# Band queries stored backwards in place of a flipped bias table, and reciprocal sums spread by GpSimd and transposes

## The chip, the cores and the metric

One core of a Trainium2 chip runs the whole kernel. The metric is the device time of one execution in microseconds (us); lower is better. The engines are named as in the profile: PE (TensorE), DVE (VectorE), ACT (ScalarE), POOL (GpSimd) and SP (SyncE, which here only issues DMAs).

## The reference, cut to what matters

The computation is two transformer blocks on 512 tokens of width 1024, all in float32. The first block has an MLA attention and a banded attention, gates, an output projection and a mixture of experts. The second has a windowed attention of 16 heads and a state-space scan. The change touches the softmax of all attentions and the relative bias of the banded one:

```
rel = (arange(64)[:, None] + 512) - arange(576)[None, :]
bias = rel_table[:, clip(rel, -256, 256) + 256]
sc = einsum('bqhd,bkhd->bhqk', q_chunk, k_band) * d ** -0.5 + bias
p = softmax(sc, axis=-1)
out = einsum('bhqk,bkhd->bqhd', p, v_band)
```

Query row q of the bias is the row before it shifted by one place, so a table with overlapping rows can be read straight from one vector.

## The kernel before, in words

Each engine has its own instruction list, written out by hand; they meet at semaphores, and an engine runs its own list strictly in order. DMAs are issued by SP for weights, and by ACT and POOL for the rest. Time runs through these stages: projections of the first block (`PE_S1`, then `PE_U`), the first attention, gates, output projection, router, mixture of experts, the projections of the second block, the second attention, convolution and state-space scan, output.

**An attention** is `attend(groups)`, with one copy in each engine's list. The first call does groups 0 (banded) and 1 (MLA), the second groups 2 and 3 (the 16 windowed heads). A group has 8 heads, taken as 4 pairs; a pair is 4 units n, one for each block of 128 queries, in the order t = 3, 0, 2, 1. A unit handles both heads of the pair and only (t+1)*128 keys, so unit n with n % 4 == 0 is the widest. For a unit:

- PE `scores(n)` (line 759) multiplies queries and keys into PSUM.
- DVE `bias_max` (line 1701) adds the bias and takes the row maximum.
- ACT `soft` (line 1336) takes the exponential and the row sums.
- PE `turn(n)` (line 769) transposes the probabilities, DVE and ACT `evict_pt` (lines 1709 and 1348) copy them to SBUF, and PE `values(n)` (line 782) multiplies them with the values.

PE issues turn(n), values(n-1), scores(n+2) in each round. When a pair is finished, DVE `invert` (line 1715) takes the reciprocals of its 8 columns of row sums, one round into the next pair. PE `spread` (line 793) then turns them into a full 128x512 tile in PSUM, by 8 matmuls: a column of reciprocals, broadcast over 64 columns, is the stationary operand and the identity moves. It is issued after scores(n+2) of the round with n % 4 == 1, or, for the last pair of a call, after everything else. DVE `normalise` (line 1721) multiplies the evicted output (ACT `evict_o`, line 1341) with it. The score and value matmuls of the next stage wait for `o_ready`.

**The bias table of group 0.** ACT's DMA at line 1400 reads it from DRAM with overlapping rows in the order of memory, so its partitions come in reverse order. PE multiplies each head's 128x512 tile with a flip matrix (line 865), DVE copies the result back (line 1845), and POOL writes the mask corner (line 2455). PE begins the attention when all eight are done. Before its own attention starts, DVE takes two weight remainders, `lo(M_G)` and `lo(M_G + 1)` (line 1675), and ACT the two rounded parts, `hi(M_G)` and `hi(M_G + 1)` (line 1323), of the first two gate tiles.

The first round of the attention also holds 16 small matmuls of the router (line 802), put after scores(0) and scores(1) and before turn(0); DVE adds their result in round 1.

After the first attention ACT (line 1410) and DVE (line 1856) split its eight output tiles into rounded part and remainder, which PE needs from line 888 on. After the second one ACT copies `RA` to `RC_r` (line 1537), POOL takes the remainders (line 2479), and PE's next column (line 663) waits for each. POOL's list during the second attention builds the biases of group 3 (lines 2488 and 2489), two heads per pair.

Of the kernel before, what the change touches and what calls it, by code (L numbers as in the profile page):

```python
# [19 lines left out]
F32 = mybir.dt.float32  # L20
# [52 lines left out]
def build(nc, xT_d, vec_d, rows_d, pos_d, rel_d, wr_d, wdt_d, pre_d, moe_d, post_d, out_d):  # L73
    ctx = ExitStack()
    with ctx:
# [32 lines left out]
        flip = sb("flip", [P, P])  # L108
# [169 lines left out]
        r_full = sem("r_full")  # L278
        o_raw = sem("o_raw")
# [58 lines left out]
        flip_full = sem("flip_full")  # L338
        flip_ev = sem("flip_ev")
# [289 lines left out]
        def _(pe):  # L629
# [114 lines left out]
            def attend(groups):  # L744
# [41 lines left out]
                def spread(pair):  # L786
                    pe.wait_ge(rs_ready, pair + 1)
                    if pair:
                        pe.wait_ge(o_ready, pair)
                    for t in range(TT):  # L790
                        for s in range(2):
                            r = pair_sums(rsinv, pair)[:, 2 * t + s:2 * t + s + 1].to_broadcast([P, 64])
                            last = mm(ps[7][64 * s:64 * s + 64, t * P:(t + 1) * P], r, ident[:, :], start=True, stop=True)
                    last.then_inc(r_full, 1)
# [66 lines left out]
            pe.wait_ge(bias_in, 16)  # L861
            for h in range(HG):
                if h >= 2:
                    pe.wait_ge(flip_ev, h)
                mm(ps[4 + h % 2][:, :], flip[:, :], bias_hc[:, h, :], start=True, stop=True).then_inc(flip_full, 1)
            pe.wait_ge(flip_ev, HG + 1)
# [365 lines left out]

        def s1_dst(i):
# [7 lines left out]
            if i < 8:  # L1241
                return [(qbT[:, i - 4, :], b[:, :])], 0.125
            if i < 12:
                return [(kbT[:, i - 8, :], b[:, :])], 1.0
            raise ValueError(i)

# [31 lines left out]
        def _(act):  # L1278
# [46 lines left out]
            def attend(groups):  # L1325
# [24 lines left out]
                for n in range(first, last_n):  # L1350
# [3 lines left out]
                    if n > first:  # L1354
                        evict_pt(n - 1)
                evict_pt(last_n - 1)
# [45 lines left out]
            hi(M_G)  # L1402
            hi(M_G + 1)
# [4 lines left out]
            for k in range(KT):  # L1408
                act.wait_ge(o_ready, PAIRS + k + 1 if k < PAIRS else 2 * PAIRS)
                A(REr[:, k, :], RH[:, k, :], ACT.Copy).then_inc(oab_hi, 1)  # L1410
# [244 lines left out]
        def _(dve):  # L1655
# [33 lines left out]
            def attend(groups):  # L1689
# [33 lines left out]
                for n in range(first, last_n):  # L1723
# [9 lines left out]
                    if n % TT == TT - 1 and n > first + TT:  # L1733
                        normalise(n // TT - 1)
                evict_pt(last_n - 1)
# [107 lines left out]
            for h in range(HG):  # L1843
                dve.wait_ge(flip_full, h + 1)
                v.tensor_copy(bias_hc[:, h, :], ps[4 + h % 2][:, :]).then_inc(flip_ev, 1)
            lo(M_G)
            lo(M_G + 1)
# [4 lines left out]
            for k in range(KT):  # L1852
# [3 lines left out]
                v.tensor_tensor(RFr[:, k, :], RH[:, k, :], REr[:, k, :].bitcast(F32), ALU.subtract).then_inc(oab_lo, 1)  # L1856
# [552 lines left out]
        def _(pool):  # L2409
# [3 lines left out]
            def link(ins):  # L2413
# [14 lines left out]
            g.memset(flip[:, :], 0.0).then_inc(flip_ev, 1)  # L2428
            pool.wait_ge(flip_ev, 1)
            link(g.affine_select(out=flip[:, :], in_=flip[:, :], compare_op=ALU.not_equal, fill=1.0, base=1 - P,  # L2430
                                 pattern=[[1, P]], channel_multiplier=1))
# [22 lines left out]
            pool.wait_ge(flip_ev, HG + 1)  # L2454
            g.memset(bias_hc[0:64, :, 448:512], NEG).then_inc(bias_ok, 1)
# [3 lines left out]
            for i in range(MAX_OVER + 1):  # L2459
                g.dma_start(exp_d[SURPLUS_ROW + i * P:SURPLUS_ROW + (i + 1) * P, :],  # L2460
                            SQ[:, :, :].rearrange("p a b -> p (a b)")).then_inc(zero_out, 16)
            pool.wait_ge(rows_ok, 1)
# [22 lines left out]
            for h in range(2 * HG):  # L2485
                if h >= HG:
                    pool.wait_ge(biased, 2 * NU + (h - HG) // 2 * 2 * TT + 2 * TT)
                link(g.tensor_scalar(RG[:, h % HG, :], delta, -float(2.0 ** (-8.0 * (h + 1) / 16)), None, ALU.mult))
                g.tensor_tensor(RG[:, h % HG, :], RG[:, h % HG, :], lnm, ALU.add).then_inc(bias_ok, 1)
            pool.wait_ge(s_full, 4 * NU)  # L2490
# [143 lines left out]
```

## Time and profile before

| What | Value |
|---|---|
| Median of 3 runs | 1323.54 us (1323.48 to 1325.14) |
| Span of the profiled execution | 1319.3 us |
| Time of the profiled execution itself | not given beside its span |
| Median minus span | 4.24 us |
| PE busy | 1231.7 us, 93% of the span |
| DVE, ACT, POOL busy | 48%, 35%, 13% |
| Line 865 (flips), PE | 181.20 to 188.89 us of the span |
| Line 793 (spreads), PE | 256 records in 16 spreads |

The profile is of one execution. Busy times of PE are modelled at their ends, so that neighbouring matmuls overlap in it; the pace is read from the starts of successive rows. A row of PE ahead of which there is no bracket had no idle time before it. One float32 matmul leaves two records, a transpose one.

### The profile page before, as it was taken

What the parts mean: (1) busy time and instruction counts of PE and PEld (TensorE: products, weight loads), DVE (VectorE), ACT (ScalarE), POOL (GpSimd) and SP (SyncE); (2) the same over time, 40 slices, a digit from 0 to 9 for tenths busy, and PEclk for the clock granted to TensorE, in tenths of its full rate; (3) what the DMA queues carried; (4) which work ended last, traced back from release to release, by engine and by line L of the source; (5) the groups of instructions that cost most, each with busy time, mean ns of one, the idle gap of its engine ahead of it and who ended that gap; (6) DMA issues with size and microseconds to landing.
All of it is one profiled execution on the core that took longest, in us unless ns stands there. A gap on an engine that the chain in (4) does not pass through costs nothing.

```text
span 1319.3 us, 17760 instructions
## 1 busy us (share of the span) xinstructions
PE 1231.7 (93%) x6946; PEld 873.0 (66%) x6946; DVE 636.4 (48%) x1180; ACT 460.8 (35%) x833; POOL 169.6 (13%) x136
## 2 busy tenths in 40 slices
PE   4899999999999989999989799999998999999995
PEld 1676566678887755444445268897656788787783
DVE  1654366554445454311111266424654675958545
ACT  3324226642222241111111252123664366564314
POOL 1200010000000000000000200700503018622003
PEclk9899999999999999999999799999999999999998
DMA  9555342113332299999999923322001222112201
GB/s 355 208 205 176 112 155 92 59 34 98 98 98 91 103 407 408 412 411 412 411 411 405 411 81 96 96 74 87 1 1 39 90 81 64 49 52 92 88 24 64
DMA packets 61633, 219.37 MB, mean 166 GB/s; under 512 B 6368, under 2 KB 6760, under 8 KB 61552
## 3 DMA queue, kind: packets, MB, share of 16 engines
q1 hardware_dynamic: 55440, 198.86, 41.4%
q10 hardware_dynamic: 3664, 10.47, 2.1%
q0 software_dynamic: 2448, 8.91, 1.7%
q8 instruction: 56, 0.92, 0.3%
q14 instruction: 25, 0.20, 0.0%
HBM read 203.52 MB, written 14.70 MB: 165 GB/s over the span
## 4 chain that ended last, share of the span: by engine, by line
PE 79%; DMA 7%; DVE 4%; ACT 4%; issue 4%; POOL 1%; SPq 0%; ACTq 0%; DVEq 0%; POOLq 0%
PE ps L663 12%; PE ps L664 12%; PE ps L665 12%; PE ps L961 6%; PE ps L942 4%; DMA ring<-in_w_moe 4%; PE ps L982 3%; PE ps L759 3%; PE ps L782 3%; PE ps L769 3%; PE ps L704 2%; PE ps L706 2%; PE ps L705 2%; PE ps L730 1%; DMA RG<-expert_rows,small 1%
## 5 line engine op out<-in xcount | busy, mean ns | idle before, releaser
L1675 DVE TENSOR_TENSOR ring_r<-ring,ring_r 128x1024 fp32r<-128x1024 f32 x115 | 143.7, 1253 | 198.3 <-ACT ring_r L1323 197.6
L1323 ACT ACTIVATE ring_r<-ring 128x1024 fp32r<-128x1024 f32 x116 | 121.2, 1052 | 204.6 <-PE ps L665 166.8
L663 PE MATMUL ps<-RB_r,ring_r 128*128 128x512 f32 x320 | 126.9, 396 | 1.1 <-DVE RH L1721 1.1
L665 PE MATMUL ps<-RB_r,ring_r 128*128 128x512 f32 x320 | 124.6, 389 | 0.0
L663 PE MATMUL ps<-RC_r,ring_r 128*128 128x512 f32 x224 | 91.1, 407 | 4.6 <-POOL RD_r L2479 3.7
L665 PE MATMUL ps<-RC_r,ring_r 128*128 128x512 f32 x224 | 87.8, 392 | 0.0
L664 PE MATMUL ps<-RD_r,ring_r 128*128 128x512 f32 x224 | 87.7, 392 | 0.0
L664 PE MATMUL ps<-RG_r,ring_r 128*128 128x512 f32 x208 | 81.1, 390 | 0.0
L1968 DVE TENSOR_SCALAR RH<-ps,small 128x256 f32<-128x256 f32 x72 | 31.5, 480 | 87.2 <-PE ps L942 87.0
L961 PE MATMUL ps<-ring,RH 128*64 128x512 f32 x308 | 73.3, 595 | 0.0
L2472 POOL DMA_INDIRECT RC<-expert_rows,small x4 | 3.8, 958 | 535.4 <-POOLq L2467 534.5
L663 PEld LDWEIGHTS ps<-RB_r,ring_r 128*128 128x128 f32 x320 | 60.1, 188 | 16.7 <-issue 4.5
L942 PE MATMUL ps<-RD_r,RC_r 128*128 128x256 f32 x288 | 67.6, 288 | 1.2 <-DVE RD_r L1948 1.2
L665 PEld LDWEIGHTS ps<-RB_r,ring_r 128*128 128x128 f32 x320 | 60.1, 188 | 12.8
L942 PE MATMUL ps<-RD_r,RG_r 128*128 128x256 f32 x288 | 66.1, 283 | 0.4 <-DVE RG_r L1957 0.4
L942 PEld LDWEIGHTS ps<-RD_r,RC_r 128*128 128x128 f32 x288 | 52.9, 191 | 13.4 <-issue 13.4
L1336 ACT ACTIVATE SB<-ps,small 128x512 f32<-128x512 f32 (+1 forms) x64 | 40.1, 630 | 43.8 <-DVE small L1701 40.3
L663 PEld LDWEIGHTS ps<-RC_r,ring_r 128*128 128x128 f32 x224 | 42.2, 188 | 19.0 <-POOL RD_r L2479 5.0
L704 PE MATMUL ps<-ring_r,RB_r 128*128 128x256 f32 x192 | 54.5, 284 | 0.0
L706 PE MATMUL ps<-ring_r,RB_r 128*128 128x256 f32 x192 | 54.3, 283 | 0.0
L2056 DVE TENSOR_TENSOR RB<-RB,ps 128x256 f32<-128x256 f32 x17 | 7.1, 420 | 95.9 <-ACT RB L1449 90.0
L942 PEld LDWEIGHTS ps<-RD_r,RG_r 128*128 128x128 f32 x288 | 52.9, 191 | 0.6 <-DVE RG_r L1957 0.6
(482 smaller groups left out, 2655.3 us busy)
## 6 DMA issues: line engine op xcount, KB each, us to landing
ring<-in_w_moe SPq DMA_DIRECT2D x108, 512.0 KB, 15.6
ring<-in_w_post SPq DMA_DIRECT2D x68, 512.0 KB, 3.6
ring<-in_w_pre SPq DMA_DIRECT2D x48, 512.0 KB, 3.6
RE<-in_w_moe SPq DMA_DIRECT2D x36, 512.0 KB, 16.2
RF<-in_w_moe SPq DMA_DIRECT2D x36, 512.0 KB, 15.6
ring<-in_w_pre SPq DMA_DIRECT2D x16, 1024.0 KB, 6.9
expert_rows<-RD ACTq DMA_DIRECT2D x15, 512.0 KB, 6.8
ring<-in_w_pre SPq DMA_DIRECT2D x3, 2048.0 KB, 16.9
```

The lines of the kernel that those rows point to most:

```text
L663: mm(out, part(m)[:, w], xh(k), start=first and k == 0, stop=False)
L664: mm(out, part(m)[:, w], xl(k), start=False, stop=False)
L665: ins = mm(out, remainder(m)[:, w], xh(k), start=False, stop=last and k == n_k - 1)
L704: mm(out, xh(k)[:, tok], hi_w, start=(k == 0), stop=False)
L706: last = mm(out, xh(k)[:, tok], lo_w, start=False, stop=(k == KT - 1))
L759: mm(ps[2 * (n % 2) + s][:, 0:w], ql(2 * p + s, t), kr(2 * p + s, w), start=True, stop=True).then_inc(s_full, 1)
L769: last = nc.tensor.transpose(ps[4 + s][:, j * P:(j + 1) * P], probs(n)[:, s, j * P:(j + 1) * P], ident[:, :])
L942: last = mm(ps[GATHER_BANKS[i]][:, k % 2 * 256:k % 2 * 256 + 256], (h2_hi, h2_lo)[s][:, t, k * P:(k + 1) * P], OHr[:, quad % 2, t, :], sta ...
L961: last = mm(ps[2 + p % 2][u * SLOTS:(u + 1) * SLOTS, :], Xg[:, buf, kk, c:c + SLOTS], moe_tile(at + 2 * s + u)[:, k * T:(k + 1) * T], star ...
L1323: A(part(m), tile, ACT.Copy).then_inc(w_hi, 1)
L1336: A(probs(n)[:, s, 0:w], ps[2 * (n % 2) + s][:, 0:w], ACT.Exp, scale=-1.0, bias=nmax(n, s), accum_out=sums(n, s)).then_inc(p_ready, 1)
L1675: v.tensor_tensor(remainder(m), arrival(m)[2], part(m).bitcast(F32), ALU.subtract).then_inc(w_split, 1)
```

## The change

The flip matrix, its matmuls and its eight copies go. Instead each block of 128 banded queries is stored backwards when it is evicted, and read backwards again when the attention's output is split. The mask corner moves to the other 64 partitions. `hi(M_G)`, `hi(M_G + 1)` are issued within ACT's attention at n = 8 and 16, and `lo(M_G)`, `lo(M_G + 1)` within DVE's at n = 10 and 18. The reciprocals are first widened on POOL to a 128x512 tile in SBUF (`widen`), and then turned by four transposes on PE.

```diff
                 def spread(pair):
-                    pe.wait_ge(rs_ready, pair + 1)
+                    pe.wait_ge(rs_wide, pair + 1)
                     if pair:
                         pe.wait_ge(o_ready, pair)
                     for t in range(TT):
-                        for s in range(2):
-                            r = pair_sums(rsinv, pair)[:, 2 * t + s:2 * t + s + 1].to_broadcast([P, 64])
-                            last = mm(ps[7][64 * s:64 * s + 64, t * P:(t + 1) * P], r, ident[:, :], start=True, stop=True)
+                        last = nc.tensor.transpose(ps[7][:, t * P:(t + 1) * P], RINV[:, t * P:(t + 1) * P], ident[:, :])
                     last.then_inc(r_full, 1)
...
-            pe.wait_ge(bias_in, 16)
-            for h in range(HG):
-                if h >= 2:
-                    pe.wait_ge(flip_ev, h)
-                mm(ps[4 + h % 2][:, :], flip[:, :], bias_hc[:, h, :], start=True, stop=True).then_inc(flip_full, 1)
-            pe.wait_ge(flip_ev, HG + 1)
             pe.wait_ge(mod_ok, 2)
             attend((0, 1))
...
+        def backwards(ap):
+            return blocks(ap)[:, :, ::-1]
...
-                return [(qbT[:, i - 4, :], b[:, :])], 0.125
+                return [(backwards(qbT[:, i - 4, :]), blocks(b[:, :]))], 0.125
...
+                    if n in (8, 16):
+                        hi(M_G + n // 8 - 1)
...
-            hi(M_G)
-            hi(M_G + 1)
...
-                A(REr[:, k, :], RH[:, k, :], ACT.Copy).then_inc(oab_hi, 1)
+                A(blocks(REr[:, k, :]), heads_out(k), ACT.Copy).then_inc(oab_hi, 1)
...
+                    if n in (10, 18):
+                        lo(M_G + n // 8 - 1)
...
-            for h in range(HG):
-                dve.wait_ge(flip_full, h + 1)
-                v.tensor_copy(bias_hc[:, h, :], ps[4 + h % 2][:, :]).then_inc(flip_ev, 1)
-            lo(M_G)
-            lo(M_G + 1)
...
-            pool.wait_ge(flip_ev, HG + 1)
-            g.memset(bias_hc[0:64, :, 448:512], NEG).then_inc(bias_ok, 1)
+            pool.wait_ge(bias_in, 16)
+            g.memset(bias_hc[64:128, :, 448:512], NEG).then_inc(bias_ok, 1)
+            pool.wait_ge(bias_ok, 1)
+            def widen(pair):
+                pool.wait_ge(rs_ready, pair + 1)
+                if pair:
+                    pool.wait_ge(r_full, pair)
+                g.tensor_copy(RINV[:, :].rearrange("p (a b) -> p a b", a=8),
+                              pair_sums(rsinv, pair).unsqueeze(2).to_broadcast([P, 8, 64])).then_inc(rs_wide, 1)
...
+            for pair in range(2 * PAIRS):
+                widen(pair)
...
                 if h >= HG:
                     pool.wait_ge(biased, 2 * NU + (h - HG) // 2 * 2 * TT + 2 * TT)
+                if h >= HG and h % 2 == 0:
+                    widen(2 * PAIRS + (h - HG) // 2)
...
+            for pair in range(3 * PAIRS, 4 * PAIRS):
+                widen(pair)
             pool.wait_ge(s_full, 4 * NU)
             remainders(RDr, RCr, RA, 16, range(KT))
```

The widening of pairs 0 to 7 stands behind POOL's nine DMAs of zeros (line 2460) in its list, that of pair 15 ahead of its eight remainders (line 2479). The two instructions that built the flip matrix go from POOL's start.

## Rows read from the trace of the kernel before

**Rows 1.** the chain that ended last, share of the span by engine (the page)

```profile
PE 79%; DMA 7%; DVE 4%; ACT 4%; issue 4%; POOL 1%; SPq 0%; ACTq 0%; DVEq 0%; POOLq 0%
```

**Rows 2.** windows: stretch, us, busy us (instructions) of each engine, clock, DMA, GB/s

```profile
194.00:278.00 84.00, 82.60 (x727) 55.31 (x725) 49.66 (x167) 51.51 (x167) 2.43 (x5) 1.00 0.20 77
...
922.00:997.00 75.00, 70.94 (x678) 45.93 (x676) 44.42 (x156) 45.90 (x150) 20.45 (x15) 1.00 0.01 2
997.00:1010.00 13.00, 9.33 (x31) 5.31 (x28) 2.30 (x4) 5.46 (x10) 10.92 (x8) 0.87 0.00 1
```

**Rows 3.** timeline of PE near line 865: start, us, engine, line, operation, [idle <-releaser]

```profile
181.20 7.69 PE L865 MATMUL ps<-ring,flip 128*128 128x512 f32 x16 [0.73 <-issue]
189.67 1.35 PE L759 MATMUL ps<-RC 64*128 64x512 f32 x8 [0.78 <-DVE ring L1845]
190.95 1.97 PE L802 MATMUL ps<-w_r,small 128*128 128x36 f32 x16
193.60 1.32 PE L769 MATMUL ps<-ident,SB 128*128 128x128 f32 x8 [0.68 <-ACT SB L1336]
```

**Rows 4.** timeline of DVE, the same stretch

```profile
189.65 2.36 DVE L1675 TENSOR_TENSOR ring_r<-ring,ring_r 128x1024 fp32r<-128x1024 f32 x2
191.93 0.69 DVE L1701 CUSTOM_DVE_ANT_0 ps<-ps,ring 128x512 f32<-128x512 f32 x1
```

**Rows 5.** timeline of POOL: the mask memset

```profile
189.68 0.52 POOL L2455 MEMSET ring<- 64x512 f32 x1 [130.70 <-DVE ring L1845]
```

**Rows 6.** timeline of PE, one spread in place, and one full turn of the MLA group

```profile
207.10 1.09 PE L793 MATMUL ps<-ident,small 128*64 128x128 f32 x16
208.12 0.88 PE L769 MATMUL ps<-ident,SB 128*128 128x128 f32 x6
...
267.68 1.04 PE L769 MATMUL ps<-ident,SB 128*128 128x128 f32 x8
```

**Rows 7.** timeline of DVE, pairs 0 and 2 of the first attention

```profile
201.67 0.19 DVE L1715 RECIPROCAL small<-small 128x8 f32<-128x8 f32 x1
...
217.68 0.43 DVE L1701 CUSTOM_DVE_ANT_0 ps<-ps,ring 128x256 f32<-128x256 f32 x1 [1.14 <-PE ps L759]
```

**Rows 8.** timeline of POOL, its copy and its 128x512 scalings

```profile
4.19 0.39 POOL L2438 COPY PTB<-PTB 8x255 f32<-8x255 f32 x1 [0.27 <-DMA PTB<-in_rel]
...
825.93 1.52 POOL L2488 TENSOR_SCALAR RG<-RH 128x512 f32<-128x512 f32 x1 [43.91 <-DVEq L2172]
...
828.91 2.35 POOL L2488 TENSOR_SCALAR RG<-RH 128x512 f32<-128x512 f32 x1
```

**Rows 9.** timeline of DVE, end of the first attention

```profile
276.12 0.19 DVE L1715 RECIPROCAL small<-small 128x8 f32<-128x8 f32 x1
...
278.23 0.69 DVE L1721 TENSOR_TENSOR RH<-RH,ps 128x512 f32<-128x512 f32 x1 [1.92 <-PE ps L793]
278.84 4.89 DVE L1856 TENSOR_TENSOR RF_r<-RH,RE_r 128x512 fp32r<-128x512 f32 x8
```

**Rows 10.** timeline of PE, end of the first attention and the gates

```profile
277.07 1.04 PE L793 MATMUL ps<-ident,small 128*64 128x128 f32 x16
279.18 0.47 PE L663 MATMUL ps<-RB_r,ring_r 128*128 128x512 f32 x1 [1.06 <-DVE RH L1721]
...
290.17 0.39 PE L888 MATMUL ps<-RE_r,ring_r 128*128 128x512 f32 x1
```

**Rows 11.** timeline of PE, end of the second attention

```profile
999.05 0.47 PE L663 MATMUL ps<-RC_r,ring_r 128*128 128x512 f32 x1 [1.85 <-POOL RD_r L2479]
```

**Rows 12.** timeline of POOL, end of the second attention

```profile
997.64 10.92 POOL L2479 TENSOR_TENSOR RD_r<-RA,RC_r 128x512 fp32r<-128x512 f32 x8 [40.91 <-ACT RC_r L1537]
```

**Rows 13.** group of the page: out<-in xcount | busy us, mean ns | idle before, releaser

```profile
L1323 ACT ACTIVATE ring_r<-ring 128x1024 fp32r<-128x1024 f32 x116 | 121.2, 1052 | 204.6 <-PE ps L665 166.8
```

**Rows 14.** timeline of ACT, first attention, unit 9

```profile
214.42 0.60 ACT L1341 ACTIVATE RH<-ps 128x512 f32<-128x512 f32 x1 [0.71 <-PE ps L782]
```

**Rows 15.** timeline of PE, first attention, the turn of unit 9

```profile
215.65 0.30 PE L769 MATMUL ps<-ident,PB 128*128 128x128 f32 x1 [0.17 <-ACT PTB L1348]
```

More of the change, by code:

```diff
@@ L107, in build @@
         upper = sb("upper", [P, P])
-        flip = sb("flip", [P, P])
         vec = sb("vec", [P, NV])
@@ L278, in build @@
         r_full = sem("r_full")
+        rs_wide = sem("rs_wide")
         o_raw = sem("o_raw")
@@ L337, in build @@
         mod_h = sem("mod_h")
-        flip_full = sem("flip_full")
-        flip_ev = sem("flip_ev")
         delta_ok = sem("delta_ok")
@@ L1230, in quad, with blocks @@
             return ap.rearrange("p (a b) -> p a b", a=4)
+        def blocks(ap):
+            return ap.rearrange("p (t c) -> p t c", t=TT)
+        def backwards(ap):
+            return blocks(ap)[:, :, ::-1]
         def s1_dst(i):
@@ L1245, in s1_dst, with heads_out @@
             raise ValueError(i)
+        def heads_out(k):
+            return blocks(RH[:, k, :]) if k < PAIRS else backwards(RH[:, k, :])
         def halves(ap):
@@ L1855, in _ @@
                     dve.wait_ge(pv_done, 2 * NPU)
-                v.tensor_tensor(RFr[:, k, :], RH[:, k, :], REr[:, k, :].bitcast(F32), ALU.subtract).then_inc(oab_lo, 1)
+                v.tensor_tensor(blocks(RFr[:, k, :]), heads_out(k), blocks(REr[:, k, :].bitcast(F32)),
+                                ALU.subtract).then_inc(oab_lo, 1)
             for i in range(KT):
@@ L2427, in _ @@
                                  pattern=[[1, P]], channel_multiplier=-1))
[L2428 to L2431, printed above, removed]
             pool.sem_inc(consts, 1)
```

## The prediction

> **What bounds the kernel now.** I read the chain that ended last first. PE holds 79% of it, and DVE, ACT and POOL together 9% [rows 1]. So an edit is worth what it takes out of PE's own sequence, or out of a wait of PE. Then I read the windows of the two attentions. In the first PE is busy for 82.60 of 84 us, in the second for 70.94 of 75 us, with DVE and ACT between 50 and 61% busy and the granted clock at 1.00 [rows 2]. Hence time taken from PE inside an attention should come back nearly whole, if the chain scores, maximum, exponential, turn moves along with it. Last I read PE's timeline around line 865, and it shows the part that is neither. The flips start at 181.20, the first scores at 189.67, and turn(0) only at 193.60 [rows 3]. The end of this stretch is DVE's: it does two remainders of 1.18 us each from 189.65 on, and its first maximum starts at 191.93, though the first scores have long been under way [rows 4]. All sums are made against this execution's span of 1319.3 us. The median of the runs is 1323.54, 4.24 more, and I carry this difference over.
>
> **Part 1, the flips go.** PE's wait at 181.20 is for the last evictions before the attention, which stay. So scores(0) and scores(1) start at 181.20 in place of 189.67. They take 1.28 us (start to next start, 189.67 to 190.95), and then come the router's matmuls, which took 1.97 us [rows 3]. PE is free for turn(0) at 181.20 + 1.28 + 1.97 = 184.45. DVE must follow. The copies and both remainders are gone from ahead of it, so its first maximum starts when head 0 is scored. I take 1.2 us after 181.20, which is nearly all of the 1.28 us, thus 182.4. Before, turn(0) came 1.67 us after that maximum (191.93 to 193.60) [rows 3, 4], which would give 184.1. PE's own queue is later, so turn(0) starts at 184.45, and the gain is 193.60 - 184.45 = 9.15 us. The router's matmuls were covered by DVE's remainders and are now bare, and that is why the gain is less than the 9.5 us that DVE alone moves. Bounds: 8.5 (a further 0.65 us, about the idle time that PE had ahead of turn(0)) and 9.5 us.
>
> What is late next here: the bias table. The flips read it at 181.20 without a DMA as releaser, so it had landed by then. The mask memset of 0.52 us [rows 5] ends by 181.8 even if it began only at 181.20, and the first maximum wants it at 182.4. POOL then clears SQ and issues its zeros, all long before the first widening is due.
>
> **Part 2, sixteen spreads.** One spread holds PE from 207.10 to 208.12, so 1.02 us. The four transposes are of the kind that PE does in `turn`: eight in 1.04 us in the MLA group (0.13 each), six in 0.88 us (0.147), eight in 1.32 us after an idle gap (0.165) [rows 3, 6]. Those busy times contain the tail of the last one, so I take 0.14 us each, 0.56 for four, with 0.52 and 0.66 as ends. That saves 0.46 us each (0.36 to 0.50). Fourteen of the sixteen lie inside a call, with PE busy on both sides, and 14 x 0.46 = 6.4 us (5.0 to 7.0).
>
> What must hold for it is that the widened tile is there. The reciprocals of pair 0 are ready at 201.67 + 0.19 = 201.86 [rows 7], and its spread begins at 207.10 [rows 6]: 5.2 us of cover. The trace has no POOL copy of this size. Its copy of 255 elements per partition took 0.39 us, and a 128x512 scaling took 1.52, or 2.35 in another case [rows 8]. The copy is the same operation with a broadcast input, as here. With about 0.1 us of it fixed (my estimate), twice the elements cost 0.7 us. I take 0.7, with 0.4 and 2.35 as ends. Any of these is hidden by 5.2 us. In the second attention POOL has a queue: widen(8) and its like stand ahead of two bias builds each, and wait for the reciprocals. But POOL is busy for only 20.45 of the 75 us there [rows 2], so each pair's builds end before the next widening is due, and what they build is wanted three pairs later. The 14 inner spreads therefore pay nothing for the new wait.
>
> The Trainium skill, "GPSIMD Engine Reference", sections 3.1 and 4.1, has one-input operations near line rate, and a case of 512 elements at 0.77 us. By that the sum would be the same within 0.1 us. The 1.52 us of the scaling, also one-input, does not agree with it. The page "SBUF — State Buffer" (Trainium skill, section "SBUF: two separate sides") says that DVE work with two SBUF inputs and POOL work that reads SBUF exclude each other for a whole instruction. The 2.35 beside 1.52 us looks like that. In an attention DVE's only such work is the two moved remainders, which stand two rounds away from a widening, so by the rule too nothing is added.
>
> **Part 3, the two last spreads.** They are bare. At the end of the first attention the reciprocals are ready at 276.31 [rows 9], PE is free at 277.07, and normalise starts 1.16 us later at 278.23, PE's next column at 279.18 [rows 9, 10]. Now the copy ends at 276.31 + 0.1 + 0.7 = 277.1, the transposes start at 277.2 and end at 277.8, and normalise can start at 277.9 to 278.0. I take 0.2 us gained. With a copy of 2.35 us it is 278.76 + 0.1 + 0.56 + 0.14 = 279.6, so 1.3 us lost. At the end of the second attention PE waits for something else: its next column starts at 999.05, released by POOL's remainder [rows 11], which began at 997.64, released by ACT's copy [rows 12]. The widening of pair 15 stands ahead of it in POOL's list, but if the reciprocals come as far ahead of the next stage as in the first attention (2.9 us, 276.31 to 279.18), they are ready at about 996.2 and the tile at 997.0. A copy of 2.35 us would end at 998.6, 1 us into the remainders. I count 0 (1.0 lost at worst).
>
> **Part 4, what moves into the attention.** ACT's `hi` (1.05 us [rows 13]) falls in round 8 after its copy and pushes unit 9's exponential and the output copy at 214.42. ACT had 0.71 us idle there [rows 14], and PE already waits 0.17 us for ACT at 215.65 [rows 15]. So a little over 0.3 us of each `hi` could show; I take 0.15 each, 0.3 in all, because ACT's next step moves forward too (ends 0 and 1.0). DVE's `lo` of 1.18 us (half of 2.36 [rows 4]) falls in round 10, just ahead of the 1.14 us for which DVE waited for PE at 217.68 [rows 7]. I count 0 (ends 0 and 1.0 for both).
>
> **Part 5, at nothing.** Four evictions write backwards, in a stage where PE's columns are long, and eight splits at the end of the first attention read in blocks, four of them backwards. DVE ends its eight at 283.73 [rows 9] and PE wants the first at 290.17 [rows 10]: 6.4 us of cover. If that cover failed, each extra us would be one on the path. POOL's start is two instructions shorter, and its other work there is short against the first loads, so nothing comes of it. Everything after the first attention, the expert weights' stream too, is started by PE's or DVE's progress, so it shifts as a block.
>
> **Sum.** 9.15 + 6.4 + 0.2 - 0.3 = 15.45 us. The span goes to 1303.9, the time to 1323.54 - 15.45 = 1308.1 us. With all small ends at their best it is 9.5 + 7.0 + 0.3 = 16.8, so 1306.7; with them at their worst 8.5 + 5.0 - 1.3 - 1.0 - 2.0 = 9.2, so 1314.3.
>
> **Rivals.**
> - *The spreads give nothing.* The turn of a pair is set by the loop scores, maximum, exponential, turn, and PE only waits longer in it. For it: PE has short waits for ACT in every pair, and 4 us of idle in the second window. Against: those waits come after scores(n), which themselves move, and PE is 98% busy in the first attention [rows 2]. Time: 9.15 + 0.2 - 0.3 = 9.05 off, 1314.5 us.
> - *The moved parts are bare.* Two `hi` and two `lo` cost their whole 1.05 and 1.18 us inside the attention, 4.5 us. For it: PE waits for ACT there already [rows 15]. Against: the idle times of DVE and ACT there [rows 7, 14]. Time: 15.75 - 4.5 = 11.25 off, 1312.3 us.
> - *Slower: the clock of the attentions.* After the gap of 1.85 us at 999.05 the granted clock fell, and the window has a mean of 0.87 [rows 2, 11]. If the attentions, whose pieces become shorter, fell to the lower level of 1.2 GHz, each us of PE work there would take two. It decides from about 16 us of such work on, a tenth of the 159 us of the two windows; with a fifth of them at the lower level it costs 32 us, and the time is 1340. Against: the clock is 1.00 through both, with their 20 transposes per pair and their small waits, and the start now has less idle time.
> - *The change doesn't do what it says* (POOL's tile comes late in every pair). It needs a copy of over 5.2 us, more than twice the longest row [rows 8]. I give it no part of its own.
>
> **Chances.** Forecast 0.70, spreads worthless 0.13, moved parts bare 0.10, slower 0.03; 0.04 for something that I don't see, three quarters of it within 0.2%. A measurement of this kernel can't tell less than about 0.2%, 2.6 us, from no change. All but the last two cases are beyond it: faster 0.93, same 0.03, slower 0.04. The range is 1305.5 to 1314.6: a us below the best end, and up to the first rival, which is also about the worst end.
>
> **What would show it.** Right: turn(0) at about 184.4; DVE's first maximum at about 182.4; spreads of 4 records and about 0.56 us; pairs of both attentions 0.46 us shorter; the first gate column 12.3 us earlier (9.15 + 7 x 0.46 + 0.2 - 0.3) and the convolution's first one 15.5. Wrong: PE waiting for POOL ahead of an inner spread, a POOL copy over 2 us, new idle time of PE for ACT in rounds 8 to 11 or 16 to 19, longer evictions in the projections, or a clock below 1.00 in an attention.

## The result, and the profile after

The changed kernel took 1304.22 us (median of 4 runs, 1301.69 to 1306.71), the kernel before 1323.91 us on the same chip. The ratio is 0.985, with a 95% interval of 0.983 to 0.987. So the gain is 19.7 us. I had forecast 15.45 us, and the time lies 1.3 us below the low end of my range. The sign, the mechanisms and their places were right; the size of one term, that of the spreads, was not. The profiled execution took 1301.69 us at a span of 1299.9 us.

The front first. PE's timeline of the changed kernel, where the flips stood (columns as in [rows 3]):

```profile
180.01 1.35 PE L757 MATMUL ps<-RC 64*128 64x512 f32 x8 [0.73 <-issue]
181.29 1.98 PE L798 MATMUL ps<-w_r,small 128*128 128x36 f32 x16
183.10 1.17 PE L767 MATMUL ps<-ident,SB 128*128 128x128 f32 x8
```

DVE's and POOL's rows beside it:

```profile
181.26 0.70 DVE L1703 CUSTOM_DVE_ANT_0 ps<-ps,ring 128x512 f32<-128x512 f32 x1 [4.76 <-PE ps L757]
...
176.88 0.52 POOL L2451 MEMSET ring<- 64x512 f32 x1 [118.71 <-DMA ring<-ext_scratch]
```

The scores start in the place of the flips, behind the same wait of 0.73 us, and the whole stage has come 1.19 us earlier (180.01 against 181.20; where that is from is told under the last two experiments). turn(0) follows the router's matmuls without a wait, as forecast, and so it is PE's own queue that sets it. It comes 10.50 us earlier, 9.31 without the shift of the stage. The first maximum starts 1.25 us after the scores, and the mask corner, released by the table's DMA, had ended 3.9 us before it.

Now the spreads. PE's timeline of the changed kernel: one spread of the banded group, one of the MLA group, and the rows around them.

```profile
195.81 0.70 PE L757 MATMUL ps<-RC 64*128 64x256 f32 x4
196.45 0.66 PE L789 MATMUL ps<-ident,RINV 128*128 128x128 f32 x4
196.94 0.82 PE L767 MATMUL ps<-ident,SB 128*128 128x128 f32 x6
...
225.88 1.13 PE L757 MATMUL ps<-RE,RD 128*128 128x256 f32 x4
226.84 0.60 PE L789 MATMUL ps<-ident,RINV 128*128 128x128 f32 x4
227.28 0.82 PE L767 MATMUL ps<-ident,SB 128*128 128x128 f32 x6
228.03 0.44 PE L780 MATMUL ps<-OTK,RF 128*64 128x128 f32 x4
```

And the MLA group in the kernel before (its banded spread is in [rows 6]):

```profile
238.21 1.13 PE L759 MATMUL ps<-RE,RD 128*128 128x256 f32 x4
239.28 1.09 PE L793 MATMUL ps<-ident,small 128*64 128x128 f32 x16
240.30 0.44 PE L769 MATMUL ps<-ident,SB 128*128 128x128 f32 x2
```

Read the distance from start to start. A spread holds PE for 0.49 us (196.45 to 196.94) in place of 1.02, and for 0.44 (226.84 to 227.28) in the MLA group. The scores ahead of it in the MLA group take 0.96 us (225.88 to 226.84) in place of 1.07, though nothing of them was edited. The turn behind a spread takes 0.75 us for six (227.28 to 228.03) in place of 0.81 [rows 6]. So a pair is shorter by more than the spread: the distance of two spreads fell from 10.45 to 9.86 us in the banded group, from 11.25 to 10.51 in the MLA group, and from 10.55 to 9.97 in the second attention.

POOL's widening, at an inner pair and at the last one of the first attention:

```profile
201.07 0.61 POOL L2459 COPY RINV<-small 128x512 f32<-128x512 f32 x1 [9.19 <-DVE small L1717]
...
261.09 0.61 POOL L2459 COPY RINV<-small 128x512 f32<-128x512 f32 x1 [7.83 <-DVE small L1717]
```

PE and DVE at the end of the first attention:

```profile
261.89 0.66 PE L789 MATMUL ps<-ident,RINV 128*128 128x128 f32 x4
263.60 0.47 PE L661 MATMUL ps<-RB_r,ring_r 128*128 128x512 f32 x1 [1.05 <-DVE RH L1723]
...
260.84 0.19 DVE L1717 RECIPROCAL small<-small 128x8 f32<-128x8 f32 x1
262.65 0.69 DVE L1723 TENSOR_TENSOR RH<-RH,ps 128x512 f32<-128x512 f32 x1 [1.62 <-ACT RH L1343]
```

normalise starts 0.76 us after the spread in place of 1.16. In this trace ACT's copy of the output releases it, and no longer the spread [rows 9]; so a spread that is shorter still would not show here.

Last, the end of the second attention, PE, POOL and DVE:

```profile
979.68 0.47 PE L661 MATMUL ps<-RC_r,ring_r 128*128 128x512 f32 x1 [2.13 <-POOL RD_r L2486]
985.52 0.62 PE L661 MATMUL ps<-RC_r,ring_r 128*128 128x512 f32 x1 [1.24 <-POOL RD_r L2486]
...
978.26 10.90 POOL L2486 TENSOR_TENSOR RD_r<-RA,RC_r 128x512 fp32r<-128x512 f32 x8 [1.75 <-ACT RC_r L1539]
...
982.81 1.53 DVE L1677 TENSOR_TENSOR ring_r<-ring,ring_r 128x1024 fp32r<-128x1024 f32 x1 [4.32 <-ACT ring_r L1325]
```

The two traces, lined up at the same instructions, give this account. Each line is how much earlier the changed kernel reaches the place than the one before.

| place | earlier by, us | gained since the line above |
|---|---|---|
| first scores (their stage starts 1.19 earlier) | 9.66 | |
| turn(0) | 10.50 | front: 9.31 without the 1.19 |
| first spread | 10.65 | 0.15, turn(0) without a wait ahead is shorter |
| last spread of the first attention | 15.19 | 4.54 |
| first gate column | 15.59 | 0.40 |
| end of the projections | 15.46 | -0.13 |
| first convolution column | 19.37 | 3.91 |
| end | 19.41 | 0.04 |

What the change did on the path is 9.31 + 0.15 + 4.54 + 0.40 + 3.91 = 18.3 us. The other 1.2 us were there before the attention.

### The profile page after: what moved, and what is told of

It reads as the page before. It is cut to its first block, busy times and chain, and to the rows that moved or that the text cites. A ratio compares the mean times of both kernels' runs of the same rounds, so it can differ in the third digit from the quotient of the medians.

```text
span 1299.9 us, 17364 instructions
## 1 busy us (share of the span) xinstructions
PE 1213.7 (93%) x6738; PEld 863.4 (66%) x6738; DVE 631.3 (49%) x1172; ACT 459.3 (35%) x833; POOL 178.9 (14%) x150
## 4 chain that ended last, share of the span: by engine, by line
PE 79%; DMA 7%; ACT 4%; issue 4%; DVE 4%; POOL 1%; SPq 0%; ACTq 0%; DVEq 0%; POOLq 0%
PE ps L661 12%; PE ps L662 12%; PE ps L663 12%; PE ps L951 6%; PE ps L932 4%; DMA ring<-in_w_moe 4%; PE ps L972 3%; PE ps L780 3%; PE ps L757 3%; PE ps L767 2%; PE ps L702 2%; PE ps L704 2%; PE ps L703 2%; PE ps L728 1%; DMA RG<-expert_rows,small 1%
```

## Experiments

All were compared in alternating runs with the kernel before; "time" is the median with the lowest and highest run. In single executions short stretches of low granted clock fall at different places, and runs of one kernel spread over up to 8 us for it; mechanisms are therefore read from the traces.

**The two halves alone.** flip_only is the changed kernel with the old spread and no widening. spread_only is the kernel before with the new one:

```diff
-                    pe.wait_ge(rs_ready, pair + 1)
+                    pe.wait_ge(ang_ok, 2 + pair + 1)
...
+                        last = nc.tensor.transpose(ps[7][:, t * P:(t + 1) * P], RINV[:, t * P:(t + 1) * P], ident[:, :])
```

> The changed kernel, but with the old spread (eight column-tiled matmuls, no widening on POOL). Theory SIZE (the forecast's mechanisms hold, and only PE's terms for the spreads were taken too small): turn(0) moves by 9.3 us beside the first scores' own shift, the two moved hi cost about 0.1 us each, so 9.2 us are saved, 1314.7 us, and the pairs are as long as before (10.44 and 11.25 us). Theory START (1.2 us of the extra gain comes from POOL's shorter start): 10.4 us saved, 1313.5 us, with the first weight column of the projections 1.2 us earlier than before. Rival (the two halves need each other): less than 8 us saved.

> The kernel before, with the flips kept and only the spread changed (widened by POOL, four transposes on PE). Theory SIZE: 0.59 us per inner spread in groups 0, 2 and 3 and 0.73 in the MLA group, 0.4 at the end of the first attention and 0.1 at the end of the second: 10 x 0.59 + 4 x 0.73 + 0.5 = 9.3 us saved, 1314.6 us. The forecast as it was written (0.46 each, 0.2 at the first end): 6.6 us saved, 1317.3 us. Theory START: no more than SIZE, since POOL's start is as before; the first projection column starts as in the kernel before.

Measured: flip_only 1315.96 us (1313.20 to 1317.68), ratio 0.993 [0.992, 0.995], spread_only 1314.01 us (1312.76 to 1314.81), ratio 0.992 [0.991, 0.993], before 1324.45. The halves are worth 8.5 and 10.4 us, together 18.9; 9.2 and 9.3 were expected by SIZE. In the trace of flip_only turn(0) is 10.44 us earlier, with the shift of its stage 1.13: 9.31, and its pairs are 10.45 and 11.25 us long, as before. In that of spread_only they are 9.86, 10.51 and 9.97 us. So the halves add, each with its own mechanism, and the larger share of what I missed is in the spreads.

**wide_matmul** asks whether it is the count of passes or the narrow tiles of the old spread that cost. Four plain float32 matmuls stand in place of the four transposes, so eight records of 128 columns' width where the old spread had 16 of 64.

```diff
-                        last = nc.tensor.transpose(ps[7][:, t * P:(t + 1) * P], RINV[:, t * P:(t + 1) * P], ident[:, :])
+                        last = mm(ps[7][:, t * P:(t + 1) * P], RINV[:, t * P:(t + 1) * P], ident[:, :], start=True, stop=True)
```

> The changed kernel, but the four transposes of a spread are plain float32 matmuls of the same operands (128 stationary columns, the identity moving). It tells apart why a spread's neighbours got faster. Theory TILE: scores before and turn after a spread are faster because no column-tiled 64-wide matmul stands between them; then with plain matmuls the neighbours stay at 0.97 (scores ahead, MLA group) and 0.75 us (turn behind). Theory PASS: they are faster because a transpose passes once where a matmul leaves two records; then they go back to 1.06 and 0.81 us. In both the spread itself goes from 0.49 to about 0.96 us, eight records at 0.12, so 14 x 0.47 = 6.6 us slower than the changed kernel under TILE, 14 x 0.53 + 4 x 0.09 = 7.8 us under PASS.

Measured: 1313.54 us (1310.21 to 1315.05), ratio 0.992 [0.990, 0.994], before 1325.00. PE's timeline of it, MLA group:

```profile
228.03 1.13 PE L757 MATMUL ps<-RE,RD 128*128 128x256 f32 x4
229.00 1.05 PE L789 MATMUL ps<-ident,RINV 128*128 128x128 f32 x8
229.89 0.82 PE L767 MATMUL ps<-ident,SB 128*128 128x128 f32 x6
230.64 0.44 PE L780 MATMUL ps<-OTK,RF 128*64 128x128 f32 x4
```

The spread itself is nearly back at its old size, 0.89 us here (229.00 to 229.89) and 1.00 in the banded group. But the scores ahead stay at 0.97 us and the turn behind at 0.75. So it isn't the one record of a transpose in place of two that makes the neighbours faster. What the old spread had and this one has not is tiles of 64 columns, twice the number of matmuls, and a stationary operand broadcast from one column; this run takes away all three at once. One place speaks for the tiles. Ahead of the bare last spread stand matmuls that write tiles of 64 columns themselves, those of the values. In the kernel before and in the changed one (the spreads that follow start at 277.07 [rows 10] and 261.89):

```profile
276.64 0.61 PE L782 MATMUL ps<-OTK,RF 128*64 128x128 f32 x8
...
261.35 0.61 PE L780 MATMUL ps<-OTK,RF 128*64 128x128 f32 x8
```

To the spread they take 0.43 us ahead of the old spread and 0.54 ahead of the new one (and of wide_matmul's): here the old spread's neighbour is the shorter. So a change of tile width between neighbours seems to be what costs. The banded scores, which use 64 rows of the array, take 0.63 to 0.64 us ahead of either. No run changes the width alone, so this is argued, not shown. By time wide_matmul is 8.2 us slower than the changed kernel, with single runs 5 us apart, which can't tell 6.6 (TILE) from 7.8 (PASS); the pairs of its trace are longer by 0.50 and 0.46 us, as TILE has it. The Trainium skill, "Perfetto Trace Analysis", section "Transposes", asks for a transpose in place of a standard matmul; the trace agrees, with 0.49 us for four against 1.00.

**spread_twice** does each of the four transposes twice, to see whether PE's time in a spread is the path's.

```diff
-                    for t in range(TT):
+                    for t in list(range(TT)) * 2:
```

> The changed kernel with each spread's four transposes made twice. It prices them in their place. Theory SIZE: PE's own sequence bounds both attentions, so every inner spread costs its full 0.49 us more (0.12 us per transpose), 14 x 0.49 = 6.9 us, and 0.5 us for the bare last one of the first attention: 7.4 us slower. By the 0.14 us of the forecast it would be 14 x 0.56 + 0.56 = 8.4 us. Rival (the loop through maximum and exponential sets a pair's length): under 2 us slower.

Measured: 1312.92 us (1308.85 to 1316.43), ratio 0.990 [0.988, 0.992]. A spread takes 0.93 us (0.87 in the MLA group), and the pairs are 10.30, 10.95 and 10.40 us long, in place of 9.86, 10.51 and 9.97: longer by just the 0.44 us that the spread is. By time it saves 12.1 us where the changed kernel saves 19.7, so it costs 7.6, with 7.4 expected. All of it is on the path, and the rival in which a pair's length is set by the loop through ACT and DVE falls.

**copy_four** repeats POOL's copy four times, to look for the cover of the new wait.

```diff
+                for turn in range(4):
+                    ins = g.tensor_copy(RINV[:, :].rearrange("p (a b) -> p a b", a=8), ...)
+                    if turn < 3:
+                        link(ins)
```

> The changed kernel with POOL's widening copy made four times in a row, 0.61 us each and about 0.1 us between, so the tile comes about 2.1 us later. If the inner spreads are covered (5.2 us from the reciprocals to the spread), only the bare last spread of the first attention shows it, about 2.0 us; at the end of the second attention PE waits for POOL's remainders, and the copies of pair 15 end within a few tenths of the time when these can begin, 0 to 0.8 us. In all 2.0 to 2.8 us slower than the changed kernel, with the 14 inner spreads at their places. Rival (the tile's time matters in every pair): 14 x 2.1 = 29 us slower.

Measured: 1305.38 us (1305.24 to 1309.68), ratio 0.987 [0.985, 0.989]. POOL and PE at the end of its first attention, and a window behind it (columns as in [rows 2]):

```profile
261.11 2.64 POOL L2460 COPY RINV<-small 128x512 f32<-128x512 f32 x4 [5.80 <-DVE small L1717]
```

```profile
263.80 0.66 PE L789 MATMUL ps<-ident,RINV 128*128 128x128 f32 x4 [1.83 <-POOL RINV L2460]
265.51 0.77 PE L661 MATMUL ps<-RB_r,ring_r 128*128 128x512 f32 x1 [1.05 <-DVE RH L1723]
```

```profile
266.00:268.00 2.00, 2.00 (x6) 1.54 (x5) 2.00 (x4) 1.99 (x4) 0.00 (x0) 0.50 0.04 8
```

The pairs' lengths don't move by more than 0.02 us: 2.64 us of POOL are hidden in 14 places. At the last spread of the first attention they are bare, the gate column comes 1.91 us later than in the changed kernel (265.51 against 263.60), and behind the longer wait the clock was granted at 0.50, where it was 1.00 in the changed kernel. At the end of the second attention the first column comes 0.46 us later, of 0 to 0.8 expected. By the medians the kernel loses only 0.1 us to the changed one (it saves 19.6), by the ratios about 2; the intervals overlap, so the 2.0 to 2.8 us expected are read from the trace alone.

**parts_ahead** puts the two `hi` and the two `lo` back ahead of the attention.

```diff
-                    if n in (8, 16):
-                        hi(M_G + n // 8 - 1)
...
+            hi(M_G)
+            hi(M_G + 1)
```

> The changed kernel, but with both hi and both lo issued ahead of the first attention again, as in the kernel before. SIZE: DVE does two lo of 1.2 us ahead of its first maximum, of which about 1.3 us were idle there once the flips are gone (it waited 4.8 us for PE), so the lo are covered if the hi that they wait for are done in time; the hi end 2 us after ACT's last eviction, so the lo end about 4.3 us after it and the first maximum comes some 2.3 us later than in the changed kernel; minus 0.2 us that the hi cost inside: 2.1 us slower than the changed kernel. Rival (the hi and lo were bare in the attention): no slower than the changed kernel.

Measured: 1308.61 us (1304.57 to 1312.29, 4 runs), ratio 0.987 [0.985, 0.989]. PE and two windows of it:

```profile
181.41 1.97 PE L798 MATMUL ps<-w_r,small 128*128 128x36 f32 x16
184.96 1.97 PE L767 MATMUL ps<-ident,SB 128*128 128x128 f32 x8 [1.58 <-ACT SB L1338]
```

```profile
184.00:187.00 3.00, 2.04 (x10) 1.71 (x10) 1.92 (x9) 2.18 (x9) 0.13 (x1) 0.50 1.02 418
187.00:190.00 3.00, 3.00 (x16) 1.59 (x18) 1.28 (x5) 1.36 (x4) 0.00 (x0) 0.50 1.02 418
```

turn(0) comes 4.83 us after the scores in place of 3.09: DVE's two `lo` hold back its first maximum by 1.90 us, and ACT's exponential with it. Then the clock is at its lower level of 1.2 GHz, and from turn(0) to the first spread it takes 15.96 us in place of 13.35. So about 1.7 us of the front's gain belong to the move, not to the flips. By time the kernel is 3.9 us slower than the changed one (it saves 15.8), with 2.1 expected; single runs lie 7.7 us apart, and the low clock was not in the sum. In its attention the first distance of spreads is 9.86 us, with `hi` in it 9.97 in the changed kernel: the first `hi` costs 0.11 us. The second costs nothing: its distance is 10.57 us in both.

**flip_built_late** is the kernel before, with GpSimd's signal for the constants ahead of the two instructions that build the flip matrix, as the first test of the 1.2 us.

```diff
+            pool.sem_inc(consts, 1)
             g.memset(flip[:, :], 0.0).then_inc(flip_ev, 1)
...
-            pool.sem_inc(consts, 1)
```

> The kernel before, with the two instructions that build the flip matrix moved behind POOL's signal that the constants are ready; nothing else. Theory START: the stages up to the first attention move by 1.2 us, 1322.7 us. Theory SIZE (the 1.2 us by which the projections began earlier is the scatter of single executions, by the places where the granted clock is at its lower level): the time is that of the kernel before within 0.1%, and the first projection column of different executions scatters by about 1 us whatever the kernel.

Measured: 1324.40 us (1323.72 to 1326.91), ratio 1.000 [0.999, 1.001]. In its trace the values' projection (PE's line 704) starts 1.29 us earlier than in the first trace of before, but its time is that of before.

**after_again, and the remainders at the end of the second attention.** rest_dve and rest_split start from the changed kernel. In rest_split VectorE takes only the odd k.

```diff
+            for k in range(KT):
+                dve.wait_ge(x_hi, 16 + k + 1)
+                v.tensor_tensor(RDr[:, k, :], RA[:, k, :], RCr[:, k, :].bitcast(F32), ALU.subtract).then_inc(x_lo, 1)
...
-            remainders(RDr, RCr, RA, 16, range(KT))
```

> The changed kernel, nothing edited. The question is how much of its 19.7 us is the change's. Theory TERMS: what its trace shows removed on the path is the flips' 9.3 us, 0.59 us on each of ten inner spreads and 0.73 us on each of four (8.8 us), 0.4 us on the last spread of the first attention and 0.2 us on that of the second, less 0.1 us for a hi: 18.6 us, and the low stretches of the granted clock fall anew in each execution, for nothing on the mean. Then the median is 18 to 19 us below the kernel before of the same rounds (ratio 0.986), single runs spread over 5 us. Rival FORECAST: the sum of 15.45 us was right and the rest was luck: ratio 0.988 or more. Rival MORE: the change does more than its terms, in each execution: ratio 0.985 or less.

> The changed kernel, with the eight remainders of the output of the second attention (RDr) computed by VectorE in place of GpSimd, right behind VectorE's last normalisation. Theory REST: behind the second attention TensorE is paced by GpSimd, 1.28 to 2.24 us for each of the eight (10.9 us in all), while VectorE is idle but for one lo. VectorE takes 0.69 us for the same shape, ScalarE's eight roundings are 0.53 us apart, and the three passes of TensorE for one k take 0.70 us at full clock: the first column starts 0.6 us earlier and ends some 4.5 us earlier. Forecast 4 to 5 us faster than the changed kernel (with its median of 1304 to 1306 us, 1299.5 to 1301.5). Rival SCATTER: TensorE's full run of matmuls only brings the granted clock down sooner or the next lo of VectorE comes late and its column waits: gain under 2 us.

> The changed kernel, with the eight remainders shared: even k on GpSimd, odd k on VectorE. Theory EXCLUSIVE: in the changed kernel's trace one of GpSimd's remainders takes 2.24 us in place of 1.28, and it is the one beside VectorE's lo (two operands from SBUF, 982.8 us); if the two engines' subtractions can't read at once, two k cost 1.28 + 0.69 = 1.97 us, TensorE's column of eight 7.9 us, against 10 now: gain 1 to 2.5 us. Theory PARALLEL: the long one is chance; two k take 1.28 us, GpSimd's four end 5.1 us after the first starts, and the column is nearly at TensorE's own pace of 5.6 us: gain 4 to 5 us, as with VectorE alone. The trace tells: GpSimd's four records sum to 5.1 us (parallel) or 7.5 us and more (exclusive).

Measured, with before at 1324.36 us: after_again 1304.59 us (1304.19 to 1304.72), ratio 0.985 [0.983, 0.987]; rest_dve 1298.37 us (1297.55 to 1301.15), ratio 0.981 [0.979, 0.983]; rest_split 1302.49 us (1298.10 to 1303.05), ratio 0.983 [0.981, 0.985]. The gain of 19.7 us is typical, not a lucky one, and FORECAST falls. The ratio lies between TERMS (0.986) and MORE (0.985), whose difference is inside its interval. DVE and PE of rest_dve:

```profile
980.41 4.90 DVE L2205 TENSOR_TENSOR RD_r<-RA,RC_r 128x512 fp32r<-128x512 f32 x8
...
981.24 0.47 PE L661 MATMUL ps<-RC_r,ring_r 128*128 128x512 f32 x1 [1.54 <-DVE RD_r L2205]
```

The first column starts 0.59 us nearer to the last normalisation and then runs at PE's own pace. From there to the next stage the kernel gains 5.4 us, and by time 6.2 us against after_again. Theory REST holds, with its 4 to 5 us a little low. This is the fastest version here by its median, 26.0 us below the kernel before. The remainders in rest_split, by tile and window (min/median/max in ns):

```profile
L2490 POOL TENSOR_TENSOR RD_r<-RA,RC_r x4: 1267/1744/1755, 977.6 to 982.3; 128x512 fp32r<-128x512 f32 x4
L2206 DVE TENSOR_TENSOR RD_r<-RA,RC_r x4: 1412/1780/1784, 978.1 to 982.8; 128x512 fp32r<-128x512 f32 x4
```

Both engines are slower than alone (1.28 and 0.69 us), and two remainders together take 1.70 us, where pure taking of turns would be 1.28 + 0.69 = 1.97 and free running 1.28. POOL's four sum to 6.4 us, between my two marks of 5.1 and 7.5. So neither theory's number was met; the rows are nearer to turns. By time rest_split gains 2.1 us against after_again, as EXCLUSIVE has it (1 to 2.5), but in its trace 3.9 us by the end of the first column, 1.5 less than with VectorE alone. The Trainium skill, "SBUF — State Buffer", section "SBUF: two separate sides", says that DVE work with two SBUF inputs and GpSimd work that reads SBUF take the shared port in turns, for a whole instruction. The trace agrees in kind, up to an overlap of 0.27 us in a pair. In the changed kernel the `lo` at 982.81 took 1.53 us in place of 1.21, and PE waited 1.24 us at 985.52 for the remainder beside it.

**Where the 1.2 us at the start are from.** before_again is the kernel before, unedited. slow_start is the changed kernel with GpSimd's signal as late as before:

```diff
+                for turn in range(2):
+                    link(g.memset(w_r[:, :, 52:64], 0.0))
             pool.sem_inc(consts, 1)
```

> The kernel before, nothing edited, for a second trace of it. In its first trace the granted clock of the stage ahead of the attentions is low once (10.2 us from 38.5 us on), and the values start at 131.52 us; in the changed kernel's it is low twice (6.8 us from 19.8 and from 40.2 us on), and they start 1.18 us earlier. Theory SCATTER: which of the two patterns falls belongs to the execution; this trace may show either, and with the second one its values start at about 130.3. Rival START: the two instructions that the flip matrix adds ahead of GpSimd's signal set the pattern; then this trace shows the first one again, with values at 131.5. The ratio is 1.000.

> The changed kernel, with two memsets of GpSimd (about 0.7 us) ahead of its signal that the constants are ready, in place of the two instructions that the flip matrix had there. Theory SCATTER: the time is the changed kernel's 1304.2 to 1304.6 us, and the values start anywhere in 130 to 131.6 us. Rival START: the signal 0.7 us later brings back the first pattern of the clock, values at 131.3 to 131.9 us, and costs about 1 us: 1305.4 us.

Measured, before at 1324.47 us: before_again 1325.80 us (1322.62 to 1327.01), ratio 1.001 [1.000, 1.002]; slow_start 1304.30 us (1301.89 to 1305.65), ratio 0.985 [0.983, 0.987]. Windows of before_again, then of the trace that the prediction was made on, both of the kernel before:

```profile
19.00:26.00 7.00, 2.99 (x16) 0.59 (x16) 3.48 (x6) 3.16 (x6) 0.00 (x0) 0.54 1.02 409
36.00:50.00 14.00, 8.98 (x33) 7.31 (x34) 13.66 (x19) 6.66 (x10) 2.34 (x1) 0.76 0.45 171
192.00:195.00 3.00, 2.63 (x12) 1.34 (x12) 1.32 (x8) 2.27 (x9) 3.00 (x7) 0.77 0.97 370
195.00:198.00 3.00, 3.00 (x24) 2.02 (x22) 1.29 (x5) 1.40 (x5) 0.20 (x1) 0.66 1.03 382
```

```profile
19.00:26.00 7.00, 2.95 (x18) 0.78 (x17) 3.46 (x5) 3.21 (x6) 0.00 (x0) 1.00 1.03 410
36.00:50.00 14.00, 8.20 (x27) 6.64 (x28) 13.76 (x19) 6.05 (x8) 2.34 (x1) 0.63 0.45 170
192.00:195.00 3.00, 2.31 (x19) 1.80 (x20) 2.56 (x11) 2.18 (x9) 3.00 (x7) 1.00 0.72 281
```

The same kernel shows both patterns of the clock at its start, and with the second one the values start at 130.30 us in place of 131.52. slow_start shows that one too (values at 129.91, just below the 130 expected) at an unchanged time. The traces of wide_matmul and spread_twice, which start like the changed kernel and have no flip matrix, show the first pattern: 1.00 in the window 19 to 26 us, 0.63 in that of 36 to 50, and values at 130.98 and 131.47 us. So each pattern occurs with and without the flip matrix. START falls: the 1.2 us are the execution's, not the change's.

## Why the prediction was wrong

- **Part 1** held. turn(0) gained 9.31 us against 9.15. The 0.16 us are mine: I took the router's busy time of 1.97 us as its length, and to the next start it is 1.81 (181.29 to 183.10). (Those are eight matmuls with 16 records, not the 16 matmuls that I wrote ahead of the prediction.) Another 0.15 us come from turn(0) being shorter with no idle time ahead of it (1.10 us to the next row, in place of 1.26), which I left out.
- **Part 2** is the step that failed, by its size. I put a spread at 0.56 us, from transposes of 0.14, and counted 0.46 us for each of 14, with 7.0 us in all as the best end. Start to start a spread takes 0.49 us (0.44 in the MLA group), and the rows beside it are shorter too: a pair gained 0.59 us, in the MLA group 0.74. For 14 that would be 10 x 0.59 + 4 x 0.74 = 8.9 us: 7.6 of the spreads themselves (10 x 0.53 + 4 x 0.58), the rest of their neighbours. Two things keep it at 8.4 us (4.54 + 3.91 less 0.1 at the last column): the first `hi`, and the last inner spread of each attention, whose saving shows only in part (in the second attention 0.29 of 0.59). Against 6.4 - 0.3 = 6.1 us forecast, 2.3 us of the missing 2.9 are here. The row that I leaned on held the answer, had I taken starts: eight transposes in the MLA group are 0.97 us to the next start, so 0.12 each. That nothing runs faster *beside* a removed piece was not argued at all; it was assumed. The traces of spread_only and wide_matmul show that it does. (DVE and ACT were 59 to 61% busy in the two windows [rows 2], not from 50 on, as I wrote; nothing hangs on it.)
- **The cover of the new wait** held: 0.61 us of POOL (0.7 forecast) behind 5 us, and 2.64 us still cost nothing.
- **Part 3**: the last spread of the first attention gained 0.40 us for 0.2, up to where ACT's copy became the last wait, and that of the second 0.1 for 0. There PE waits for POOL's remainder, as forecast.
- **Part 4**: the first `hi` cost 0.11 us and the second nothing, for 0.15 each, a `lo` nothing. But I did not see what the move itself bought: left ahead of the attention they would have made ACT late for turn(0), 1.7 us. As Part 1 reasoned from the changed order, the sum was right without it.
- **Part 5** held: from the first gate column to the end of the projections the distance is that of before within 0.13 us.
- **The rivals.** "The spreads give nothing" falls by spread_twice and spread_only; "the moved parts are bare" by Part 4's numbers. "Slower: the clock of the attentions" did not come in this trace: windows of 184 to 264 us and of 900 to 978 us show 1.00. But a small piece of it shows in two of the changed kernel's three traces, after_again and slow_start: at the start of the second attention the clock fell, for about 1.4 us (told below).
- **The carry-over from the profiled execution.** Terms of 18.3 us against 19.7 us by time (19.8 in the second comparison). The halves by time sum to 18.9. This trace of before had a span of 1319.3 us, and its second trace 1324.2 us. I took the whole distance of 4.24 us to the median as a constant. In the later runs, time less span was 1.7 to 2.1 us; the rest was that this execution was a good one. Part of the remaining 1.4 us may be the stretch of low clock behind the stall ahead of turn(0), told below. Against it stands the like stretch in the second attention, in two of the changed kernel's three traces and in none of the three of the kernel before (slow_start and flip_built_late counted with them). The interval of the ratio is wider than the 1.4 us (±2.4 us), and their cause stays open.

## What to carry to other kernels

Take the cost of a short piece on PE from start to start of successive rows, and ask what its neighbours do once it is gone: here full-width matmuls took up to 0.10 us longer beside matmuls into tiles of 64 columns. A sum worked out on one execution should carry only the part of the distance to the median that every run has. After a change that shortens a stage, look at what paces the next one: here GpSimd's eight remainders held PE, and moving them to an idle VectorE was worth another 6 us.

## What the hardware showed that I had not expected

- Eight float32 matmuls into tiles of 64 columns (1.02 us) cost as much as four into 128 columns (1.00 us; 0.89 in the MLA group). Beside them the full-width matmuls ahead take 0.10 us more (MLA group) and the transposes behind 0.06, and matmuls that themselves write 64 columns 0.11 less. Four transposes of the same size cost 0.49 us.
- A stall of PE at the start of an attention can be paid twice. In before_again the granted clock was 0.77 and 0.66 in the two windows behind the stall of 0.68 us ahead of turn(0), in flip_built_late 0.60 in the first of them, in parts_ahead 0.50 behind 1.58 us. From turn(0) to the first spread before_again lost 1.56 us to the first trace of the same kernel, where the clock stayed at 1.00. It also stayed there in spread_only, which has the same stall, so the stall alone doesn't decide it. In the nine traces that have no stall there (three of them of the changed kernel, slow_start counted), it stayed at 1.00. At the start of the second attention every version waits 1.57 us for ACT, and the clock fell behind it in 5 of the 14 traces: after_again, slow_start, wide_matmul, spread_twice and parts_ahead. PE's first turn there and the window behind it, in the changed kernel's first trace and then in after_again:

```profile
899.69 1.32 PE L767 MATMUL ps<-ident,SB 128*128 128x128 f32 x8 [1.57 <-ACT SB L1338]
...
899.00:902.00 3.00, 2.30 (x14) 1.34 (x14) 1.72 (x8) 2.60 (x9) 0.00 (x0) 1.00 0.33 134
```

```profile
899.49 1.80 PE L767 MATMUL ps<-ident,SB 128*128 128x128 f32 x8 [1.57 <-ACT SB L1338]
...
899.00:902.00 3.00, 2.51 (x10) 1.80 (x12) 1.41 (x7) 2.40 (x9) 0.00 (x0) 0.62 0.29 117
```

From there to the first spread of that attention it takes 13.65 us at 1.00, and 15.0 to 15.2 where the clock fell. That the removed stall gives time back in some executions is argued from these traces, not shown by a run that isolates it.
- Storing and reading blocks backwards, on ACT and DVE alike, cost nothing that the traces show: ScalarE's eight splits take 0.62 us each and VectorE's 0.68 in both kernels, four of them backwards in the changed one.
- GpSimd's 128x512 copy from a broadcast input took 0.61 us; its subtraction of the same size 1.28 us alone, 1.74 beside VectorE's, and 2.24 beside a VectorE subtraction of twice the size.
